# A hybrid encoder layer on one core: the gate table's twelve blocks written out, its stores issued by ScalarE

## The chip, the cores and the metric

The kernel runs on one core of a Trainium2 chip. The metric is the device time of one execution in microseconds (us), lower is better. Before the change it is 3697.43 us, the median of 3 runs (3694.62 to 3698.45).

## The reference

One layer: two token mixers on a shared input projection, a gated merge, and then a retrieval layer of single-neuron experts (PEER) with 128 x 128 experts. The change touches only the last part. For a token with its 8 heads of 16 chosen experts the reference computes

```python
gate = jax.nn.softmax(best_s, axis=-1)
u = expert_u[experts]
v = expert_v[experts]
act = jax.nn.gelu(jnp.einsum('pd,phkd->phk', xb, u), approximate=False)
return jnp.einsum('phk,phkd->pd', (gate * act.astype(f32)).astype(xb.dtype), v)
```

There are 1024 tokens and the width is 1024. An expert's number is i x 128 + j, with i and j from the two halves of the key.

## The kernel before

It runs through phases: front, mixer, merge, route, rows, experts, finish. Of the 1024 tokens, 768 are "dense": for them the kernel computes the activation of every expert (`ahead_dram`, 128 rows of 128 experts) and a table of gates that is nearly all zeros (`gates_dram`, 128 x 128 x 768 floats), and the expert phase later multiplies the two and applies `expert_v`. The other 256 tokens are "sparse": their chosen rows are gathered one by one by indirect DMAs.

The change lies in `rows_phase` (line 1739). All of its stretch runs these streams together:

- **The rows of `expert_u`**, 128 in number. POOL issues the load of a row (512 KB, L1686), ScalarE (ACT) copies the high part (`cut_high`, L1711), VectorE (DVE) subtracts to get the low part (`cut_low`, L1715), TensorE (PE) multiplies in three passes (L460 to L462), 48 matmuls for a row in two halves h = 0 and 1, ACT applies Gelu to each half (`gelu`, L1721), and SP stores that half, 192 KB, into `ahead_dram` (`store`, L1691). The Gelu of a half waits until the store of the same half of the row before has landed (`ge_out[h]`), for there is one buffer `ge` for each half.
- **The sparse tokens**: POOL issues gathers of 128 rows of 4 KB (L1637) into a ring of four buffers, and DVE multiplies each with the tokens (L1654).
- **The gate table**, in twelve blocks of 64 tokens, each of 16 groups of 4 tokens. For a group DVE makes a one-hot of j for four tokens (L2011) and the weighted one-hot of i for three of them (L2015). ACT makes the fourth (`last_row`: L1878, then L1880), one group ahead. PE multiplies the two for each token (L2083, 8 instructions for a group) and then 6 matmuls of a row of `expert_u`. ACT copies the result out of PSUM into `stage` (L1903; the profile calls that memory `arena`). A block takes two rows of `expert_u` with it, numbers 48 to 71 in all. The store of a finished block into `gates_dram` (L1862) is 4096 KB in runs of 64 tokens, 256 bytes.

The rows phase has three parts: eight tiles with the search of the best experts (rows 0 to 47), the twelve blocks, and then the remaining rows 72 to 127 (`rest`), of which the first 23 pairs run with eight gathers each.

The order inside a block on ACT is written by hand: for each group the fourth one-hot of the group after it, then the copy out; the Gelu of the row's first half after the fifth group of its eight (k == 4), the Gelu of its second half after the first group of the next eight (k == 0), and for the last row of the block after the sixteenth group, in the order copy out, Gelu, then the next block's first `last_row`. At the start of a block ACT also waits for the store of the block two before (`st_out`).

On every engine the twelve blocks are a hardware loop of six turns of two blocks each: `blocks` (line 1789) on POOL and PE, `act.Fori` with `link.enter` and `link.leave` on ACT (line 1928) and DVE (line 2041), `sp.Fori` on SP (line 1855). The addresses and the values waited for are computed from the loop's register at every use. SP's list for a block is four `ahead_dram` stores (two rows, two halves), then a wait for the copy out of the block's last group and the block's store:

```python
sp.wait_ge(g_cp.sem, g_cp.done(b * NG + (NG - 1)))
sp.dma_start(gv[:, :, bass.ds(b * BT, BT)],
             stage[:, :, half * BT:(half + 1) * BT]).then_inc(st_out[half].sem, 16)
```

Of the kernel before, what the change touches and what calls it, by code (L numbers as in the profile page):

```python
# [1723 lines left out]
ROWS_BLOCK = 2  # L1724
# [9 lines left out]
def rows_phase(nc, TV, TI, arena, iT, jT, wT, gates, h2hi, h2lo, expert_u, ahead, few, table, keep):  # L1734
# [9 lines left out]
    BT = 64  # L1744
    G = 4
    NG = BT // G
    PER = NG // ROWS_BLOCK
    CH = 2 * KD // PER
    NB = TD // BT
# [4 lines left out]
    with ExitStack() as ctx:  # L1754
# [4 lines left out]
        stage = arena[:, :].rearrange("p (i t) -> p i t", t=2 * BT)  # L1759
# [18 lines left out]
        hot_done, g_mm, g_cp = Steps(sem("hot_done"), 2), Steps(sem("g_mm"), 2), Steps(sem("g_cp"), 2)  # L1778
        st_out = [Steps(sem(f"st_out{i}"), 1, 16) for i in range(2)]
        gv = gates.rearrange("i j t -> j i t")  # L1780

        def tiles(eng, body):

            for t in range(FEW + 1):
                body(t, max(t - FEW, 0) if t >= FEW else DT + t, t < FEW, t == FEW)
            with eng.Fori(FEW + 1, TT) as t:
                body(t, t + (-FEW), False, False)

        def blocks(eng, body):

            with eng.Fori(0, NB // 2) as turn:
                body(turn)

        def rest(eng, body):

            with eng.Fori(0, WITH) as turn:
                body(turn, False, True)
            with eng.Fori(WITH, TURNS - 1) as turn:
                body(turn, False, False)
            body(TURNS - 1, True, False)  # L1800

        with nc.Block() as block:
            @block.gpsimd
            def _(pool):
# [24 lines left out]
                def block_rows(turn):  # L1829
                    for half in range(2):  # L1830
# [3 lines left out]
                        for i in range(RING):  # L1834
                            few.gather(pool, table, batch, half, i)
                            if i % 2 == 0:
                                load(b * 2 + (ROW_GATE + 2 + i // 2), i // 2)

                blocks(pool, block_rows)

                def rest_rows(turn, last, rows):
# [9 lines left out]
            @block.sync  # L1851
            def _(sp):
                with sp.Fori(0, ROW_GATE) as r:
                    A.store(sp, r, r)
                with sp.Fori(0, NB // 2) as turn:
                    for half in range(2):
                        b = turn * 2 + half
                        for j in range(ROWS_BLOCK):
                            A.store(sp, b * 2 + (ROW_GATE + j), b * 2 + (ROW_GATE + j))

                        sp.wait_ge(g_cp.sem, g_cp.done(b * NG + (NG - 1)))
                        sp.dma_start(gv[:, :, bass.ds(b * BT, BT)],  # L1862
                                     stage[:, :, half * BT:(half + 1) * BT]).then_inc(st_out[half].sem, 16)
                with sp.Fori(ROW_REST, NKEYS) as r:
                    A.store(sp, r, r)
                for half in range(2):
                    sp.wait_ge(st_out[half].sem, st_out[half].done(NB // 2 - 1))
                for out in A.ge_out:
                    sp.wait_ge(out.sem, out.done(NKEYS - 1))

            @block.scalar
            def _(act):
                link = Chain(act, sem("act_rows"))

                def last_row(b, gi):
                    at = bass.ds(b * BT + (gi * G + G - 1), 1)
                    w = less[:, bass.ds(b * NG + gi, 1)]
                    link(act.activation(away[:, gi % 2], K.iota[:, :], ACT.Abs, bias=iT[:, at], scale=-1.0))  # L1878
                    act.wait_ge(g_mm.sem, g_mm.free(b * NG + gi))
                    act.activation(row[:, gi % 2 * G + G - 1], away[:, gi % 2], ACT.Relu, bias=wT[:, at], scale=w).then_inc(hot_last.sem, 1)  # L1880

                def tile(t, at, sparse, first):
                    for j in range(R):
                        r = t * R + j
                        A.cut_high(act, r + 1, 1 - j % 2, (t * (R // 2) + (j + 1) // 2) * 16 + 16)
                        for h in range(2):
                            A.gelu(act, r, h)
                        if j == R // 2:
                            act.wait_ge(bm_done, t + 1)
                            act.activation(best[:, :, :], best[:, :, :], ACT.Exp).then_inc(be_done, 1)  # L1890

                def block_rows(turn):
                    for half in range(2):
                        b = turn * 2 + half

                        act.wait_ge(st_out[half].sem, st_out[half].free(turn))
                        last_row(b, 0)
                        for gi in range(NG):
                            if gi + 1 < NG:
                                last_row(b, gi + 1)  # L1900
                            at = half * BT + gi * G
                            act.wait_ge(g_mm.sem, g_mm.done(b * NG + gi))
                            act.activation(stage[:, :, at:at + G], pg[gi % 2][:, :, :].rearrange("p t i -> p i t"), ACT.Copy).then_inc(g_cp.sem, 1)  # L1903
                            j, k = divmod(gi, PER)
                            r = b * 2 + (ROW_GATE + j)
                            if k == 0 and gi:
                                A.gelu(act, r + (-1), 1)
                            if k == 1:
                                A.cut_high(act, r + 1, 1 - j, (b + (ROW_GATE // 2 + j)) * 16 + 16)
                            if k == 4:  # L1910
                                A.gelu(act, r, 0)
                        A.gelu(act, b * 2 + (ROW_GATE + ROWS_BLOCK - 1), 1)

                def rest_rows(turn, last, rows):
                    for p in range(2):
                        r = turn * 2 + (ROW_REST + p)
                        if not (last and p):
                            A.cut_high(act, r + 1, 1 - p, (turn + (ROW_REST // 2 + p)) * 16 + 16)
                        for h in range(2):
                            A.gelu(act, r, h)  # L1920
                    if last:
                        act.wait_ge(few.row_used.sem, few.row_used.done(ITEMS - 1))
                        act.activation(few.dot[:, :, :], few.dot[:, :, :], ACT.Gelu).then_inc(act_done, 1)

                A.cut_high(act, 0, 0, 16)
                tiles(act, tile)
                act.wait_ge(turned_done, DT)
                with act.Fori(0, NB // 2) as turn:
                    link.enter(turn, 2 * NG)
                    block_rows(turn)  # L1930
                link.leave(NB // 2)
                rest(act, rest_rows)

            @block.vector
            def _(dve):
                link = Chain(dve, sem("dve_rows"))
# [66 lines left out]
                def block_rows(turn):  # L2003
                    for half in range(2):
                        b = turn * 2 + half
                        for gi in range(NG):
                            u = gi % 2

                            dve.wait_ge(g_mm.sem, g_mm.free(b * NG + gi))
                            four = jT[:, bass.ds(b * BT + gi * G, G)]  # L2010
                            dve.tensor_tensor(col[:, u * G:(u + 1) * G], K.iota[:, None, :].to_broadcast([P, G, P]),  # L2011
                                              four[:, :, None].to_broadcast([P, G, P]), ALU.is_equal)
                            for q in range(G - 1):
                                at = bass.ds(b * BT + (gi * G + q), 1)
                                step = dve.tensor_scalar(row[:, u * G + q], K.iota[:, :], iT[:, at], wT[:, at], ALU.is_equal, ALU.mult)  # L2015
                            step.then_inc(hot_done.sem, 1)
                            if gi % RING == RING - 1:
                                i = gi // RING
                                few.dot_row(dve, b * RING + (ITEMS_BEST + i), i)
                            j, k = divmod(gi, PER)  # L2020
                            if k == 4:
                                A.cut_low(link, b * 2 + (ROW_GATE + j + 1), 1 - j)
# [15 lines left out]
                    tile(turn + (FEW + 1), turn + 1, False, False)  # L2038
                link.leave(DT - 1)
                turned(TT - 1, DT - 1)  # L2040
                with dve.Fori(0, NB // 2) as turn:
                    link.enter(turn, 2 * ROWS_BLOCK)
                    block_rows(turn)
                link.leave(NB // 2)
                with dve.Fori(0, WITH) as turn:
                    link.enter(turn, 2)
                    rest_rows(turn, False, True)
# [10 lines left out]
            def _(pe):  # L2058
# [35 lines left out]
                tiles(pe, tile)  # L2094
                turn_over(TT - 1)
                blocks(pe, block_rows)
                rest(pe, rest_rows)

# [282 lines left out]
```

## Time and profile before

| | us |
|---|---|
| median of 3 runs | 3697.43 |
| the profiled execution, its own time | 3682.71 |
| its span | 3681.0 |
| PE busy | 3360.2 |
| DVE busy | 2580.8 |
| ACT busy | 1181.7 |
| the twelve blocks, first to last PE instruction of the table | 1627.9 to 2060.5 |

The profiled execution is 14.7 us shorter than the median of the runs. Times in the trace are counted from the start of its span. An engine's idle time is put down to what ended it: another engine's instruction, a DMA, or "issue", which is time in which the profile shows nothing that the engine waited for. An instruction on a queue (SPq, ACTq) is the issue of a DMA, not the transfer.

### The profile page before, as it was taken

To read this page: it belongs to the slowest core of one execution; us is meant where nothing else is said; L and a number is where in the kernel's file an instruction comes from. 1 tells how busy PE (TensorE), PEld (TensorE's weight loads), DVE (VectorE), ACT (ScalarE), POOL (GpSimd) and SP (SyncE) were. 2 spreads that over 40 slices of the span, in tenths; PEclk is the share of its full clock that TensorE was granted. 3 is DMA by queue.
4 is the path that set the end of the run, shared out by engine and by line. 5 is a ranking of instruction groups with operands and counts; after the bars stand their busy time and mean duration, and the time that the engine had idled before them with its cause. 6 is when DMAs were issued, how large, how long until landed. Compare 5 with 4: busy or idle time off the path is not lost. (4 is left out here: it accounts for less than half of the span.)

```text
span 3681.0 us, 58605 instructions
## 1 busy us (share of the span) xinstructions
PE 3360.2 (91%) x18867; PEld 3062.0 (83%) x18867; DVE 2580.8 (70%) x4927; ACT 1181.7 (32%) x2017; POOL 873.6 (24%) x904
## 2 busy tenths in 40 slices
PE   5997999799698899998989799998799999999996
PEld 4997888788587899998888799998688888888885
DVE  6435777455588788988878566661777777777775
ACT  3003555433222222247667322222222222222220
POOL 1000111111000011122212266661333333333331
PEclk8998999899899899999999899999899999999998
DMA  6622222253110344448888899993887787787875
GB/s 251 220 92 97 85 77 87 88 153 120 58 44 28 102 152 144 136 140 226 226 221 222 260 343 346 339 338 112 290 289 291 282 295 286 283 295 282 293 286 192
DMA packets 435649, 742.47 MB, mean 202 GB/s; under 512 B 224368, under 2 KB 275744, under 8 KB 432416
## 3 DMA queue, kind: packets, MB, share of 16 engines
q1 hardware_dynamic: 335200, 369.32, 30.4%
q0 software_dynamic: 98624, 369.14, 29.0%
q10 hardware_dynamic: 1664, 2.13, 0.2%
q8 instruction: 68, 1.11, 0.1%
q14 instruction: 93, 0.76, 0.1%
HBM read 607.30 MB, written 133.19 MB: 201 GB/s over the span
## 5 line engine op out<-in xcount | busy, mean ns | idle before, releaser
L460 PE MATMUL apab<-h2hi,auhib 128*128 128x384 f32 x2048 | 709.7, 347 | 64.2 <-DVEq L60 42.4
L461 PE MATMUL apab<-h2lo,auhib 128*128 128x384 f32 x2048 | 690.1, 337 | 0.0
L462 PE MATMUL apab<-h2hi,aulob 128*128 128x384 f32 x2048 | 689.8, 337 | 0.0
L1637 POOL DMA_INDIRECT vrow<-in_expert_v,fw_now x256 | 318.8, 1245 | 723.5 <-DVE acc L1663 710.4
L460 PEld LDWEIGHTS apab<-h2hi,auhib 128*128 128x128 f32 x2048 | 389.7, 190 | 71.9 <-ACT ageb L1721 31.6
L461 PEld LDWEIGHTS apab<-h2lo,auhib 128*128 128x128 f32 x2048 | 389.6, 190 | 0.0
L462 PEld LDWEIGHTS apab<-h2hi,aulob 128*128 128x128 f32 x2048 | 388.5, 190 | 0.0
L1721 ACT ACTIVATE ageb<-apab 128x384 f32<-128x384 f32 x256 | 125.7, 491 | 683.4 <-PE apab L462 633.9
L2245 PE MATMUL eheld<-vhi,Hhi 128*128 128x512 f32 x768 | 303.3, 395 | 31.8 <-DVE Hlo L2203 31.8
L1663 DVE SCALAR_TENSOR_TENSOR acc<-vrow,fw_share,acc 128x1024 f32<-128x1024 f32 x256 | 327.3, 1279 | 0.0
L1686 POOL DMA_DIRECT2D aurb<-in_expert_u x128 | 71.7, 560 | 1050.2 <-DVEq L60 732.7
L2217 DVE TENSOR_TENSOR acc<-acc,evo 128x512 f32<-128x512 f32 x192 | 132.2, 688 | 257.3 <-PE evo L2247 257.3
L2179 ACT ACTIVATE Hhi<-gr 128x768 fp32r<-128x768 f32 x128 | 108.5, 848 | 606.4 <-DVE gr L2195 606.4
L2246 PE MATMUL eheld<-vlo,Hhi 128*128 128x512 f32 x768 | 300.4, 391 | 0.0
L2247 PE MATMUL eheld<-vhi,Hlo 128*128 128x512 f32 x768 | 299.6, 390 | 0.0
L2245 PE MATMUL evo<-vhi,Hhi 128*128 128x512 f32 x768 | 298.8, 389 | 0.0
L2246 PE MATMUL evo<-vlo,Hhi 128*128 128x512 f32 x768 | 298.8, 389 | 0.0
L2247 PE MATMUL evo<-vhi,Hlo 128*128 128x512 f32 x768 | 298.7, 389 | 0.0
L2083 PE MATMUL gp<-grow,gcol 128*128 128x128 f32 x1536 | 213.6, 284 | 42.9 <-ACT grow L1880 33.3
L2083 PEld LDWEIGHTS gp<-grow,gcol 128*128 128x128 f32 x1536 | 203.1, 197 | 54.2 <-issue 40.3
L1715 DVE TENSOR_TENSOR aulob<-aurb,auhib 128x1024 fp32r<-128x1024 f32 x128 | 156.5, 1223 | 114.4 <-ACT auhib L1711 108.9
L1654 DVE SCALAR_TENSOR_TENSOR urow<-urow,nx 128x1024 f32<-128x1024 f32 x128 | 156.6, 1226 | 68.3 <-DMA urow<-in_expert_u_rows,fw_now 58.8
(309 smaller groups left out, 7376.4 us busy)
## 6 DMA issues: line engine op xcount, KB each, us to landing
aurb<-in_expert_u POOLq DMA_DIRECT2D x128, 512.0 KB
vraw<-in_expert_v SPq DMA_DIRECT2D x128, 512.0 KB, 3.3
ahead_dram<-ageb SPq DMA_DIRECT2D x256, 192.0 KB
gates_dram<-arena SPq DMA_DIRECT2D x12, 4096.0 KB, 24.4
ga<-ahead_dram SPq DMA_DIRECT2D x128, 384.0 KB, 5.4
gr<-gates_dram SPq DMA_DIRECT2D x128, 384.0 KB, 6.0
late<-in_w_ada SPq DMA_DIRECT2D x48, 512.0 KB, 6.4
gw<-in_w_in POOLq DMA_DIRECT2D x8, 1408.0 KB
```

What stands on the lines that cost most here:

```text
L460: pe.matmul(out, lhi, rhi, start=(k == 0), stop=False)
L461: pe.matmul(out, lhi, rlo, start=False, stop=False)
L462: return pe.matmul(out, llo, rhi, start=False, stop=(k == n - 1))
L1637: pool.indirect_dma_start(self.ring[i], None, table, bass.IndirectOffsetOnAxis(ap=self.now[:, h, i:i + 1], axis=0)).then_inc(self.row_in[i ...
L1654: dve.scalar_tensor_tensor(self.ring[i], self.ring[i], 1.0, self.h2[:, i % FEW], ALU.mult, ALU.mult, accum_out=flat[:, bass.ds(n, 1)]).the ...
L1663: dve.scalar_tensor_tensor(at, self.ring[i], flat[:, bass.ds(n - ITEMS, 1)], at, ALU.mult, ALU.add).then_inc(self.row_used.sem, 1)
L1715: link(link.eng.tensor_tensor(self.ulo[:, p], self.ur[:, p], self.uhi[:, p].bitcast(F32), ALU.subtract), self.ulo_done.sem)
L2083: step = pe.matmul(pg[u][:, q], col[:, u * G + q], row[:, u * G + q], start=True, stop=True)
L2217: dve.tensor_tensor(place_of(u), place_of(u), vo[u // 2 % BANKS][:, :], ALU.add).then_inc(vo_add.sem, 1)
L2245: pe.matmul(bank[:, :], hi, vhi[:, m, ds], start=fresh, stop=False)
L2246: pe.matmul(bank[:, :], hi, vlo[:, m, ds], start=False, stop=False)
L2247: step = pe.matmul(bank[:, :], lo, vhi[:, m, ds], start=False, stop=(q == Q - 1 and (dh == 1 or final)))
```

## The change

Three edits. `blocks`, used by POOL and PE, becomes a Python loop, so the six turns are written out as straight code and `turn` is a number: addresses and values waited for are constants. ACT, DVE and SP get the same, and the chain of ACT and DVE drops its `enter` and `leave`. The store of a finished block moves from SP's list to ACT's, between the copy out of the block's last group and the Gelu of its last half row.

```diff
         def blocks(eng, body):
 
-            with eng.Fori(0, NB // 2) as turn:
+            for turn in range(NB // 2):
                 body(turn)
...
                     A.store(sp, r, r)
-                with sp.Fori(0, NB // 2) as turn:
+                for turn in range(NB // 2):
                     for half in range(2):
                         b = turn * 2 + half
                         for j in range(ROWS_BLOCK):
                             A.store(sp, b * 2 + (ROW_GATE + j), b * 2 + (ROW_GATE + j))
 
-                        sp.wait_ge(g_cp.sem, g_cp.done(b * NG + (NG - 1)))
-                        sp.dma_start(gv[:, :, bass.ds(b * BT, BT)],
-                                     stage[:, :, half * BT:(half + 1) * BT]).then_inc(st_out[half].sem, 16)
...
                             if k == 4:
                                 A.gelu(act, r, 0)
+                        act.wait_ge(g_cp.sem, g_cp.done(b * NG + (NG - 1)))
+                        act.dma_start(gv[:, :, bass.ds(b * BT, BT)],
+                                      stage[:, :, half * BT:(half + 1) * BT]).then_inc(st_out[half].sem, 16)
                         A.gelu(act, b * 2 + (ROW_GATE + ROWS_BLOCK - 1), 1)
...
-                with act.Fori(0, NB // 2) as turn:
-                    link.enter(turn, 2 * NG)
-                    block_rows(turn)
-                link.leave(NB // 2)
+                blocks(act, block_rows)
...
-                with dve.Fori(0, NB // 2) as turn:
-                    link.enter(turn, 2 * ROWS_BLOCK)
-                    block_rows(turn)
-                link.leave(NB // 2)
+                blocks(dve, block_rows)
```

## Rows read from the trace of the kernel before

**Rows 1.** The page's first line.

```profile
span 3681.0 us, 58605 instructions
```

**Rows 2.** Busy time in stretches of 73 us, one turn: engines, granted clock, DMA share, GB/s.

```profile
1700.00:1773.00 73.00, 65.49 (x450) 63.59 (x451) 59.15 (x148) 51.61 (x111) 16.07 (x14) 0.97 0.84 225
1992.00:2065.00 73.00, 68.11 (x468) 66.53 (x469) 58.02 (x145) 51.66 (x109) 15.55 (x15) 0.98 0.85 228
```

**Rows 3.** Waits, 1627 to 2065 us: total us, times, longest.

```profile
PEld gp L2083 <- issue: 40.3, 12, 5.5
PE gp L2083 <- ACT grow L1880: 33.3, 11, 5.2
DVE gcol L2011 <- issue: 14.1, 5, 3.0
ACT gaway L1878 <- issue: 13.2, 5, 3.3
```

**Rows 4.** Timeline of PE: start, length in us, and in brackets the idle time before.

```profile
1700.48 2.07 PE L2083 MATMUL gp<-grow,gcol 128*128 128x128 f32 x8 [4.56 <-ACT grow L1880]
1736.00 1.15 PE L2083 MATMUL gp<-grow,gcol 128*128 128x128 f32 x8 [1.77 <-ACT grow L1880]
1772.48 2.07 PE L2083 MATMUL gp<-grow,gcol 128*128 128x128 f32 x8 [4.16 <-ACT grow L1880]
1809.16 1.94 PE L2083 MATMUL gp<-grow,gcol 128*128 128x128 f32 x8 [1.77 <-ACT grow L1880]
```

**Rows 5.** Timeline of ACT around the ends of blocks and at a ninth group.

```profile
1660.82 0.60 ACT L1903 ACTIVATE arena<-gp 128x512 f32<-128x512 f32 x1 [1.33 <-PE gp L2083]
1661.87 0.49 ACT L1721 ACTIVATE ageb<-apab 128x384 f32<-128x384 f32 x1 [0.45 <-PE apab L462]
...
1681.32 0.49 ACT L1721 ACTIVATE ageb<-apab 128x384 f32<-128x384 f32 x1
...
1699.11 0.40 ACT L1878 ACTIVATE gaway<-iota,iT 128x128 f32<-128x128 f32 x1 [2.66 <-issue]
1699.75 0.49 ACT L1880 ACTIVATE grow<-gaway,wT,gless 128x128 f32<-128x128 f32 x1 [0.23 <-ACT gaway L1878]
```

**Rows 6.** Granted clock and busy time after a turn's end.

```profile
1698.00:1710.00 12.00, 9.52 (x59) 9.53 (x60) 7.92 (x20) 7.61 (x17) 0.00 (x0) 0.86 0.98 216
```

**Rows 7.** Register instructions of DVE's sequencer for the weighted one-hots: ns min/median/max.

```profile
L2015 DVEq FUSED_REGOPS  x576: 46/69/81, 1626.4 to 2057.4; - x192
```

**Rows 8.** Instruction fetch, 1627 to 2065 us: packets, MB, share of the DMA engines.

```profile
q14 instruction: 56, 0.46, 0.3%
```

**Rows 9.** DMAs that ACT issues in the merge phase: ns min/median/max.

```profile
L1255 ACTq DMA_DIRECT2D mwr<-in_w_branch x4: 424/492/565, 719.5 to 721.0; - x4
```

**Rows 10.** Timeline of SP, DMA issues: start and how long SP was in it.

```profile
1663.13 0.39 SPq L1862 DMA_DIRECT2D gates_dram<-arena  x1
1673.70 12.10 SPq L1691 DMA_DIRECT2D ahead_dram<-ageb  x1
...
1697.22 0.38 SPq L1862 DMA_DIRECT2D gates_dram<-arena  x1
1711.97 4.42 SPq L1691 DMA_DIRECT2D ahead_dram<-ageb  x1
...
2064.06 0.38 SPq L1862 DMA_DIRECT2D gates_dram<-arena  x1
2066.70 28.14 SPq L1691 DMA_DIRECT2D ahead_dram<-ageb  x1
```

**Rows 11.** The gate table's stores, L1862.

```profile
DMA to landing us min/median/max: 23.4/24.4/24.9
```

**Rows 12.** Timelines of ACT and PE after the last block.

```profile
2097.35 0.98 ACT L1721 ACTIVATE ageb<-apab 128x384 f32<-128x384 f32 x2 [25.70 <-DMA ahead_dram<-ageb]
2097.89 0.69 PE L460 MATMUL apab<-h2hi,auhib 128*128 128x384 f32 x1 [19.40 <-ACT ageb L1721]
```

**Rows 13.** Busy time, clock, DMA share and GB/s after the last block.

```profile
2065.00:2095.00 30.00, 13.50 (x78) 13.18 (x77) 11.32 (x18) 1.93 (x3) 11.00 (x12) 0.79 1.08 321
2095.00:2120.00 25.00, 22.11 (x114) 22.11 (x115) 13.02 (x19) 5.92 (x9) 11.77 (x12) 0.84 0.69 214
2120.00:2484.00 364.00, 355.04 (x2013) 349.45 (x2012) 250.80 (x372) 82.39 (x126) 241.30 (x248) 1.00 0.96 343
```

## The prediction

> **What bounds the kernel now.** I read first the page, whose span is 3681.0 us [rows 1], then the busy times of the stretch of the twelve blocks, turn by turn. There PE is busy 65.5 of 73 us, DVE 59.2 and ACT 51.6; the last turn, with no jump back behind it, has 68.1 [rows 2]. So PE is the bound of this stretch, and what can be won is its idle time and the time it runs at the lower clock. Then I read the waits of the stretch. PE was held 11 times by ACT's one-hot, 33.3 us in all, and ACT and DVE each stood five times for "issue", 13.2 and 14.1 us [rows 3]: five is the number of jumps back in six turns. The timeline puts them in place: PE's gap at the start of a turn is 4.56 and 4.16 us, and between the two blocks of a turn 1.77 us [rows 4]. Six gaps of 1.77 are 10.6 us, which leaves 22.7 us for five jumps, 4.54 each, in line with the two shown. ACT's own line shows why a jump costs more: after the last Gelu it has 2.66 us of "issue" ahead of the next one-hot, and PE starts when that and the weighted one-hot are done [rows 5].
>
> Last I read SP's line and what follows the last block. The store of a block takes SP only 0.38 us, but the next store of SP stands in its issue until 1685.80, which is 22.7 us after the block's store was issued, in the other block 19.2 us (1716.39 less 1697.22), and after the last one 30.8 us (2094.84 less 2064.06) [rows 10]; the block's store lands after 24.4 us [rows 11]. So the issue of SP's next DMA ends shortly before the long store does. Within the blocks nobody waits for SP. After the last block somebody does: ACT's Gelu waits 25.70 us for the landing of that delayed store and PE 19.40 us for the Gelu [rows 12].
>
> **The change, part by part.**
>
> *Jumps back.* Five gaps of 4.54 us become gaps like those between blocks, 1.77 us, since the same instructions stand there: 5 x 2.77 = 13.9 us. The same gap is the price if nothing but the jump goes, and I see no way for it to be longer than now for that reason.
>
> *The clock after the gap.* The first eight table instructions after a jump take 2.07 us instead of 1.15 [rows 4], and the granted clock of the 12 us around a turn's start is 0.86 [rows 6]: PE, having stood 4.56 us, ran a while at the lower of its two levels, 1.2 instead of 2.4 GHz. What it costs: the block from 1736.00 to the gap before 1772.48 (at 1768.32) takes 32.32 us; the one from 1700.48 to 1734.23 takes 33.75, the one from 1772.48 to 1807.39 takes 34.91. That is 1.4 and 2.6 us, say 1.94 for each of five, 9.7 us. But at 1809.16 the clock fell behind a gap of only 1.77 us (1.94 us for eight), in one of six such places, so I count five sixths: 8.1 us. Bounds 0 and 9.7.
>
> *Constants.* The register instructions go (69 ns each on DVE's sequencer [rows 7]). DVE shows its idle time as waits for others or for the jumps, and PE is the bound: 0 us, covered by DVE's own work. If the cover were gone DVE would still be issued ahead of its need. POOL and SP have long waits in this stretch and get nothing from it.
>
> *ACT's new work.* Twelve times ACT waits for its own copy and issues a DMA before the Gelu. The copy ends at 1661.42 and the Gelu starts at 1661.87 [rows 5], so 0.45 us are free. A DMA issued by ACT took 0.49 us [rows 9], and a wait for ACT's own instruction before cost 0.23 us [rows 5]: 0.72 less 0.45 is 0.27 us, which delays the Gelu, behind it the first one-hot of the next block, and PE. Twelve times: 3.2 us lost. Bounds: 0, and 0.565 + 0.23 = 0.8 us with nothing free, 9.5 us. SP loses the same wait and issue, at no gain.
>
> *After the last block.* If SP's short stores no longer stand behind the long one, the wait of 19.40 us goes, with about 2 us of low clock. What is late next is DMA: between 2065 and 2095 its engines are full (share 1.08 by this view), and from 2120 to 2484, where the gathers end, the share is 0.96 with PE losing 9 us [rows 13]. The bytes to be moved are the same. The stall wasted only what the engines left idle behind it, 25 us at 0.69 instead of 0.96 or so, 25 x 0.27 = 6.8 us. I take 7 us; the bounds are 0 (SP stands all the same) and 21 us (DMA is no limit). Near the DMA bound, because 0.96 is nearly full. The Trainium skill (DMA: Bandwidth & Descriptors, Issuing engines are not separate DMA queues) says that DMAs from several engines run on the same 16 DMA engines and that issuing from several saves only the initiating sequencer's time, which is usually small. By that rule this part is worth 0 and the time would be 7 us above mine. Here that time is no small one: SP was 28.14 us in one issue [rows 10].
>
> Sum: 13.9 + 8.1 - 3.2 + 7 = 25.8 us. Against the profiled execution of 3682.7 that is 3656.9; the median of the runs stands 14.7 us above that execution, and I give the forecast against it: 3697.4 - 25.8 = 3671.6, so **3672 us**. Its own range: the least is 13.9 + 0 - 9.5 + 0 = 4.4 us won, the most 13.9 + 9.7 - 0 + 21 = 44.6, which is 3653 to 3693.
>
> **The rivals.**
>
> *A, ends slower: the long store holds SP's short ones from ACT's list too.* What stands in the issue for 12 and 28 us may be the list of SP alone or something that SP and ACT share. The trace has no long store issued by one engine and a short one by the other, so it can't say. If shared, the order has become worse: now SP issues the last half row before the block's store, afterwards ACT issues the block's store first. The store of that half row then stands until 19.2 to 22.7 us after ACT's issue at about 1661.65, so until 1680.9 or 1684.3, and lands 2.5 us later (2097.35 less 2094.84 [rows 10, 12]): 1683.4 or 1686.8. The Gelu that needs its buffer starts now at 1681.32 [rows 5]. ACT would stand 2.1 or 5.5 us in every block; PE feels it less what ACT is ahead (about 1 us) but falls to the lower clock behind the longer ones (1.9 us). I take 3 us for each of 11 blocks, 33 us, bounds 0 and 5.5 + 1.9 = 7.4, 81 us; and the 7 us of the tail don't come. 3672 + 7 + 33 = 3712 us. It decides from the point where PE loses more than 18.8 / 11 = 1.7 us in a block. For it speaks that SP's wait follows the long store's progress and not SP's own work. Against it that the known wait is of one list behind itself. The Trainium skill (DMA: Bandwidth & Descriptors, Queues, rings and completion order) says that SP and ACT each own a ring on every DMA engine, but no descriptor generator of their own; by the first half A falls, by the second it can stand, and no row here shows it.
>
> *B: straight code has to be fetched too.* In the loop 56 packets of instructions came, 0.46 MB [rows 8], about 9 in a turn, and only at the jump was anybody seen standing for "issue". Straight code needs about as many bytes on ACT and DVE and more on PE, whose code now stays. If the fetch is merely late at other places, the first two terms are lost and the time is 3697.4 + 3.2 - 7 = 3694 us. Against it: inside a turn, whose code is fetched in order, these rows show no such wait.
>
> *C: the moved store does nothing and the rest holds.* 3679 us; it lies inside the range of the forecast.
>
> **How the numbers follow.** The forecast (C inside it) 0.56, A 0.34, B 0.10. A measurement of this kernel can tell about 0.2%, 7.4 us, from no change. The forecast is nearly always beyond that on the fast side. A, between 3679 and 3760, gives faster in one of six, the same in one of five, and slower else. B is mostly the same. Faster: 0.54 + 0.05 + 0.02 = 0.61; slower 0.22 + 0.02 = 0.24; the same 0.15. The range has to hold most of both signs: from 3654, where nearly all of the forecast's range starts, to 3724, which takes in the greater part of A.
>
> **What would show it.** Right: ACT and DVE have no "issue" waits in the twelve blocks; PE's gaps at the eleven block ends are about 2.0 us; the granted clock of the stretch is above 0.97; a block takes some 34.4 us; SP's issues stay below 1 us while ACT's long store is under way; PE's wait of 19.4 us is gone and the DMA share stays near 0.96 through 2120. A is shown by SP issues of 10 to 20 us, by ACT's Gelu of the ninth group waiting for a landing of `ahead_dram`, and by PE gaps in the tenth or eleventh group. B is shown by "issue" waits within blocks. The forecast is wrong if ACT itself stands in the issue of its DMA for more than 1 us, or if the tail stays.

## The result and the profile after

The changed kernel takes 3642.91 us, the median of 4 runs (3638.2 to 3650.44), before 3697.78 us (4 runs). The ratio is 0.9866, 95% interval 0.9841 to 0.9891: 54.9 us faster by the medians. The forecast was 3672 us, within 3654 to 3724. The side was right, the size was a little under half of what came, and the time lies below the range.

The profiled execution of after takes 3640.8 us, 41.9 us less than the one of before (3682.7). Where that lies is read from two groups, the table's matmuls and the first matmuls of the expert phase; the last pair of each row is its first and last start. Before, first:

```profile
L2245 PE MATMUL eheld<-vhi,Hhi x768: 389/389/767, 2597.0 to 3645.1; 128*128 128x512 f32 x192
```

and after (line numbers are lower by 6 below the edits):

```profile
L2077 PE MATMUL gp<-grow,gcol x1536: 272/275/422, 1633.7 to 2031.4; 128*128 128x128 f32 x192
L2239 PE MATMUL eheld<-vhi,Hhi x768: 387/389/764, 2555.6 to 3603.3; 128*128 128x512 f32 x192
```

The table's matmuls ran from 1627.9 to 2060.5 before. So there are three stretches. Up to the first block after is 5.8 us later, in code that the change doesn't touch (over all runs here this start lies anywhere between 1628 and 1656 us). The **twelve blocks** went from 432.6 to 397.7 us, 34.9 less. **From the last block to the expert phase** it went from 536.5 to 524.2 us, 12.3 less. The rest is equal within 0.5 us. The two stretches of the forecast, 18.8 and 7 us there, gave 47.2 us together.

The waits within the blocks, 1634 to 2032 us (total us, times, longest), answer to [rows 3]:

```profile
ACT arena L1900 <- PE gp L2077: 82.1, 156, 2.0
DVE gcol L2008 <- PE gp L2077: 41.7, 47, 2.2
PE gp L2077 <- DVE grow L2012: 18.3, 12, 2.9
PE gp L2077 <- issue: 1.5, 1, 1.5
DVE gcol L2008 <- DVE aulob L1715: 0.5, 1, 0.5
```

Every "issue" wait of ACT and DVE is gone. PE is held for 2.9 us before the first block, once for 0.3 us inside it, and for 1.5 us at each of the eleven block ends (one of them stands in the row with "issue"). The same view of before has two rows more that matter, which I hadn't used:

```profile
PE gp L2083 <- DVE grow L2015: 9.5, 24, 3.2
DVE gcol L2011 <- DVE aulob L1715: 8.0, 24, 0.3
```

These are short waits inside the blocks. Without the one of 3.2 us ahead of the first block PE lost 6.3 us in 23 of them, and DVE stood 0.33 us behind each of its 24 subtractions (L1715), where it waits for its own completion. After, one of each is left, in the first block.

PE's busy time in all of the stretch, before and after, with the granted clock and the DMA share:

```profile
1628.00:2061.00 433.00, 393.39 (x2685) 382.28 (x2685) 353.16 (x884) 302.65 (x643) 95.73 (x85) 0.96 0.80 214
```

```profile
1634.00:2032.00 398.00, 381.07 (x2686) 370.87 (x2685) 350.79 (x884) 302.38 (x643) 67.02 (x84) 1.00 0.86 233
```

The same 2685 matmuls were busy for 12.3 us less, mostly since PE never fell to 1.2 GHz here (clock 0.96, now 1.00). Not all of it is clock: a kernel below (ACT's straight code alone) keeps the short waits at a clock of 0.99, and PE is busy 382.9 us there, so some 2 us of the 12.3 can come without the lower clock. The 34.9 us are these 12.3 us of busy time and 22.6 us of gaps: 5 x (4.54 - 1.51) = 15.2 at the jumps, 6 x 0.26 = 1.6 at the other block ends, and some 6 us of short waits.

A block's end on ACT, and PE's next gap, answering to [rows 4, 5], with DVE's last one-hots for the next block:

```profile
1666.35 0.60 ACT L1900 ACTIVATE arena<-gp 128x512 f32<-128x512 f32 x1 [1.34 <-PE gp L2077]
1666.98 0.40 ACTq L1910 DMA_DIRECT2D gates_dram<-arena  x1
1667.05 0.85 DVE L2012 TENSOR_SCALAR grow<-iota,iT,wT 128x128 f32<-128x128 f32 x3
1667.48 0.49 ACT L1721 ACTIVATE ageb<-apab 128x384 f32<-128x384 f32 x1 [0.53 <-PE apab L462]
1667.87 0.39 ACT L1875 ACTIVATE gaway<-iota,iT 128x128 f32<-128x128 f32 x1
1668.30 0.49 ACT L1877 ACTIVATE grow<-gaway,wT,gless 128x128 f32<-128x128 f32 x1
```

```profile
1668.89 1.13 PE L2077 MATMUL gp<-grow,gcol 128*128 128x128 f32 x8 [1.52 <-DVE grow L2012]
```

The copy ends at 1666.95, the issue starts 0.03 us later and is over at 1667.38, ahead of the Gelu: it fits into the time that was free. Between the two one-hot steps no wait is left; before there were 0.23 us [rows 5]. The profile names DVE's one-hot as what released PE, but by the same rows DVE's was over at 1667.90 and ACT's at 1668.79, 0.1 us before PE starts. An experiment below shows that it was ACT.

SP's short stores over the whole kernel, min/median/max in ns, and the long store's time to landing, answering to [rows 10, 11]:

```profile
L1691 SPq DMA_DIRECT2D ahead_dram<-ageb x256: 332/332/369, 1228.1 to 2524.0; - x128
```

```profile
DMA to landing us min/median/max: 23.7/26.5/76.4
```

No short store stood in its issue for more than 0.369 us. The last long store took 76.4 us to land. And behind the last block, to be read beside [rows 13]:

```profile
2035.00:2060.00 25.00, 25.00 (x146) 25.00 (x145) 16.33 (x24) 5.87 (x9) 14.77 (x16) 1.00 1.10 377
2060.00:2120.00 60.00, 58.40 (x334) 57.46 (x333) 40.47 (x62) 13.75 (x21) 40.87 (x41) 1.00 1.05 380
```

PE is busy for all of the first 25 us while the DMA engines move 377 GB/s, where before, with PE standing, they moved 321.

### The profile page after: what moved, and what is told of

Its sections match the earlier page's. It is cut to its first block and busy times, and to the rows that moved or that the text cites. A ratio compares the mean times of both kernels' runs of the same rounds, so it can differ in the third digit from the quotient of the medians.

```text
span 3639.1 us, 56033 instructions
## 1 busy us (share of the span) xinstructions
PE 3352.0 (92%) x18867; PEld 3052.5 (84%) x18867; DVE 2578.6 (71%) x4927; ACT 1181.3 (32%) x2017; POOL 865.3 (24%) x904
## 5 line engine op out<-in xcount | busy, mean ns | idle before, releaser
L2077 PE MATMUL gp<-grow,gcol 128*128 128x128 f32 x1536 | 206.5, 278 | 19.8 <-DVE grow L2012 18.3
L1715 DVE TENSOR_TENSOR aulob<-aurb,auhib 128x1024 fp32r<-128x1024 f32 x128 | 156.4, 1222 | 89.2 <-ACT auhib L1711 85.8
```

The source lines that it names most:

```text
L1715: link(link.eng.tensor_tensor(self.ulo[:, p], self.ur[:, p], self.uhi[:, p].bitcast(F32), ALU.subtract), self.ulo_done.sem)
L2077: step = pe.matmul(pg[u][:, q], col[:, u * G + q], row[:, u * G + q], start=True, stop=True)
```

## The experiments

All kernels keep what is computed. "Blocks" is from the first to the last start of a table matmul, "to experts" from there to the first start of the expert phase's matmul; both are read from the two groups as above. The kernels came in three lots, each on one chip; before was timed beside them at 3696.1 us (13 runs), 3690.3 (1) and 3701.4 (6). Where a kernel ran once, its total also holds the start of the blocks, which lies between 1629.5 and 1654.2 us in those traces; its stretches say more than its total.

**Before again.** No edit.

> The kernel before once more, to have its trace from the chip of the three other runs. The profiled execution of before was 14.7 us shorter than the median of its runs, the one of after was not. If the stretches of the trace are stable, the twelve blocks take 432 to 434 us again and the stretch from the last table instruction to the first matmul of the expert phase 535 to 540 us. If the missing 13 us (54.9 measured against 41.9 between the two traces) lie in these stretches, one of them comes out 10 us longer.

```profile
L2083 PE MATMUL gp<-grow,gcol x1536: 271/275/574, 1629.5 to 2058.7; 128*128 128x128 f32 x192
L2245 PE MATMUL eheld<-vhi,Hhi x768: 389/389/763, 2592.9 to 3640.0; 128*128 128x512 f32 x192
```

Blocks 429.2 us, to experts 534.2 us, and 3677.58 us in all, while 13 other executions of the same kernel on this chip took 3689.89 to 3702.68. So the traces of before are stable within 3 us in each stretch, and the profiled execution is again the shortest, by 12 to 25 us. The missing 13 us are in neither trace. They stay open. Against this trace of before, the blocks of after are 31.5 us shorter instead of 34.9.

**Straight code alone.** SP keeps the long stores.

```diff
                             A.store(sp, b * 2 + (ROW_GATE + j), b * 2 + (ROW_GATE + j))
 
+                        sp.wait_ge(g_cp.sem, g_cp.done(b * NG + (NG - 1)))
+                        sp.dma_start(gv[:, :, bass.ds(b * BT, BT)], ...)
...
-                        act.wait_ge(g_cp.sem, g_cp.done(b * NG + (NG - 1)))
-                        act.dma_start(gv[:, :, bass.ds(b * BT, BT)], ...)
```

> The straight code alone: SP keeps the stores of the table. Theory 1 (the two parts of the change act apart, jumps and constants within the blocks, the moved store behind them): the twelve blocks take about 397 us as in after, SP's short stores stand 10 to 23 us in their issue, PE has the stall of about 19 us after the last block, and the stretch from there to the expert phase is back at 536 us; about 12 us slower than after, 3655 us. Theory 2 (a part of what was won within the blocks comes from SP's short stores being free): the twelve blocks take 403 us or more.

Measured: 3663.12 us (4 runs), ratio to before 0.9904 (0.9886 to 0.9922). Blocks 397.6 us, to experts 541.2. SP's line and PE's and ACT's after the last block:

```profile
2038.82 0.43 SPq L1862 DMA_DIRECT2D gates_dram<-arena  x1
2042.68 28.22 SPq L1691 DMA_DIRECT2D ahead_dram<-ageb  x1
```

```profile
2073.65 0.69 PE L460 MATMUL apab<-h2hi,auhib 128*128 128x384 f32 x1 [19.18 <-ACT ageb L1721]
```

All of the gain in the blocks comes from the straight code, and the stall behind them stays as it was. Theory 1 holds. SP's short store is free at 2070.90, 32.1 us after the long store's issue, which lands after 33.7 us. By the medians the straight code alone is worth 33.0 us of the 3696.1.

Here the stretch to the experts is 4.7 us longer than in the first trace of before. What differs behind the stall is PE's wait for the signal of DVE's subtraction (L60 is the helper that gives it). It is 6.6 us in before (2098 to 2560 us), 12.8 in this kernel (2074 to 2540) and 13.6 in after (2031 to 2520), in the same order:

```profile
PE apab L460 <- DVEq L60: 6.6, 10, 2.0
PE apab L460 <- DVEq L60: 12.8, 14, 2.4
PE apab L460 <- DVEq L60: 13.6, 16, 2.2
```

So against this kernel the moved store brings 541.2 less 524.2, 17.0 us of the stretch, and 20.2 us by the medians: about the whole stall.

**The moved store alone.** The loops stay.

```diff
-                        sp.wait_ge(g_cp.sem, g_cp.done(b * NG + (NG - 1)))
-                        sp.dma_start(gv[:, :, bass.ds(b * BT, BT)], ...)
...
+                        act.wait_ge(g_cp.sem, g_cp.done(b * NG + (NG - 1)))
+                        act.dma_start(gv[:, :, bass.ds(b * BT, BT)], ...)
                         A.gelu(act, b * 2 + (ROW_GATE + ROWS_BLOCK - 1), 1)
```

> The moved store alone, in the loops as before. Theory 1: the twelve blocks take 433 to 436 us (ACT's issue adds 0 to 0.3 us a block), the stall of 19 us after them is gone and the stretch to the expert phase takes 524 us; 3683 to 3688 us. Theory 2: the blocks are shorter than 430 us. Rival A of the prediction would show SP issues of 10 to 20 us here as well; the trace of after has none above 1.2 us, so I expect none.

Measured: 3688.07 us (10 runs), ratio 0.9983 (0.9963 to 1.0002). To experts 524.4 us as expected, but blocks 438.6 us, 2.6 above the expectation and 6 to 9 more than in the two traces of before. ACT at a block's end:

```profile
1661.69 0.60 ACT L1900 ACTIVATE arena<-gp 128x512 f32<-128x512 f32 x1 [1.33 <-PE gp L2083]
1662.45 0.41 ACTq L1910 DMA_DIRECT2D gates_dram<-arena  x1
1662.99 0.49 ACT L1721 ACTIVATE ageb<-apab 128x384 f32<-128x384 f32 x1 [0.70 <-PE apab L462]
1663.38 0.39 ACT L1875 ACTIVATE gaway<-iota,iT 128x128 f32<-128x128 f32 x1
1664.00 0.49 ACT L1877 ACTIVATE grow<-gaway,wT,gless 128x128 f32<-128x128 f32 x1 [0.23 <-ACT gaway L1875]
```

```profile
1664.72 1.15 PE L2083 MATMUL gp<-grow,gcol 128*128 128x128 f32 x8 [2.02 <-ACT grow L1877]
```

In the loop the issue begins 0.16 us after the copy instead of 0.03, the Gelu comes 0.25 us later than before, and PE's gap is 2.02 instead of 1.77 us. This is the cost that the prediction had for the whole change (0.27 us a block). At the five jumps it is more: gaps of 5.29 to 5.46 us, 5.35 in the mean instead of 4.54, for ACT's "issue" there is 3.1 to 3.3 us instead of 2.3 to 3.3. That makes 5 x 0.81 + 6 x 0.23 = 5.4 us in all. The cost is real in a loop and absent in straight code. So the two parts are not independent: alone, the move isn't clear of no change.

**Eleven stores by SP, the last by ACT.**

```diff
+                        if b < NB - 1:
+                            sp.wait_ge(...); sp.dma_start(...)
...
+                        if b == NB - 1:
+                            act.wait_ge(...); act.dma_start(...)
```

> Straight code, SP issues eleven of the stores and ACT only the last. Theory 1: SP's short stores stand 10 to 23 us in the blocks and nobody waits for them, the blocks take 397 us, and since the last store is ACT's the stall after the blocks is gone, 524 us to the expert phase: the same as after, 3643 us. If stores standing in the blocks cost something, it is between after and the straight code alone.

Measured: 3643.96 us (4 runs), ratio 0.9858 (0.9841 to 0.9875), the same as after. Blocks 397.7 us, to experts 521.4. SP stood 10.8 to 13.0 us in the issue of a short store behind each of its long ones and nobody waited for it. The whole worth of the move, 19.2 us against the straight code alone (3663.12), lies in the last store.

**Which engine's straight code?** Three kernels, all with the moved store, to be compared with its 438.6 us. PE, POOL and SP keep their loops.

```diff
-                with act.Fori(0, NB // 2) as turn:
-                    link.enter(turn, 2 * NG)
-                    block_rows(turn)
-                link.leave(NB // 2)
+                for turn in range(NB // 2):
+                    block_rows(turn)
```

> The moved store, and only ACT's twelve blocks as straight code; PE, DVE, POOL and SP keep their loops. Theory 1a (PE's gap at a jump is ACT's chain: its jump, then its one-hot): the gaps at the jumps shrink from 4.5 us to at most what DVE and PE need for their own jumps, about 2.5 to 3.5 us, since DVE's 3.0 us of issue lie ahead of its one-hots; gaps between the blocks of a turn 1.5 us. The blocks take 422 to 428 us. Theory 1b (all engines' jumps end together): they stay above 4 us.

> The moved store, and only DVE's twelve blocks as straight code. Theory 1a: the gaps at the jumps stay at 4.2 to 5.2 us and those between blocks at 1.8, for ACT is last there, but PE's short waits of 0.27 us for DVE's one-hots inside the blocks vanish, and so do DVE's own waits of 0.33 us behind cut_low, worth 0.5 us a block: 427 to 430 us. If the constants of DVE are worth nothing, 433 us or more.

> The moved store, ACT and DVE as straight code; PE, POOL and SP keep their loops. If PE's own jump is hidden in the 1.5 us gap and its register instructions cost nothing, the blocks take 397 to 400 us as in after. If PE's jump shows, gaps of 1.5 us become 2.5 to 3.5 us at five places: 402 to 408 us.

One run each. ACT alone: 3645.32 us, blocks 408.6 us, better than expected (422 to 428). DVE alone: 3684.34 us, blocks 432.0 us, a little above the expectation. Both: 3633.95 us, blocks 399.6 us, as in after within 2 us. The waits of the first two:

```profile
PE gp L2081 <- DVE grow L2013: 17.6, 29, 3.2
PE gp L2081 <- ACT grow L1877: 11.6, 7, 1.7
DVE gcol L2009 <- issue: 10.0, 4, 3.0
DVE gcol L2009 <- DVE aulob L1715: 8.0, 24, 0.3
```

```profile
PE gp L2081 <- ACT grow L1877: 38.0, 11, 5.3
PE gp L2081 <- DVE grow L2015: 3.3, 2, 3.0
DVE gcol L2011 <- DVE aulob L1715: 0.5, 1, 0.5
```

With ACT straight no gap at a block's end is above 2.44 us, although DVE still jumps and stands 3 us for "issue" there. DVE runs ahead of PE, so most of its jump is covered. With DVE straight the gaps at the jumps stay at 4.9 to 5.3 us, but PE's short waits within the blocks vanish with DVE's own. PE's jump, POOL's and SP's cost next to nothing together. Of the 40.9 us between the blocks of the loops with the moved store and those of after, ACT's straight code brings 30.0, about three quarters, and DVE's on top of it 9.0.

**Four blocks a turn.** Three turns, two jumps back instead of five, all registers as before.

```diff
-            with eng.Fori(0, NB // 2) as turn:
-                body(turn)
+            with eng.Fori(0, NB // 4) as turn:
+                for part in range(2):
+                    body(turn * 2 + part)
```

> The moved store, all engines in loops of three turns of four blocks: two jumps back instead of five, all register addresses as before. If a jump costs 2.8 us of gap and 1.9 us of low clock, three fewer make the blocks 14 us shorter than with two blocks a turn, about 419 us; gaps of 1.77 us stay between blocks and so do the waits of 0.27 us. If the price lies in the fetch of the loop's code, it grows with the body and the two jumps left cost more than 4.5 us each.

Measured, one run: 3683.12 us, blocks 421.5 us. Three jumps fewer make the blocks 17.1 us shorter, 5.7 us for a jump, where the prediction had 2.77 + 1.94 = 4.7; with the moved store in the loop a jump's gap is 3.35 us longer than another block's end (5.35 and 2.00). The two that are left cost gaps of 4.9 and 5.3 us, no more than the 5.3 to 5.5 with the shorter body, so no growth of the price with the body's length shows, from two to four blocks. What a jump waits for the runs don't say. The rows of the waits:

```profile
PE gp L2086 <- ACT grow L1878: 28.2, 11, 5.3
ACT gaway L1876 <- issue: 5.9, 2, 3.2
```

**After again.** No edit, as the neighbour of the last three.

> The changed kernel once more, beside the two that follow on the same chip: 3640 to 3650 us, the twelve blocks 397.7 us, 524 us from them to the expert phase.

3644.67 us (4 runs, 3637.24 to 3667.72), blocks 397.7, to experts 521.9.

**The next block's one-hot ahead.** ACT makes it before the last copy, the store and the last Gelu of a block.

```diff
-                        last_row(b, 0)
+                        if b == 0:
+                            last_row(b, 0)
                         for gi in range(NG):
                             if gi + 1 < NG:
                                 last_row(b, gi + 1)
+                            elif b + 1 < NB:
+                                last_row(b + 1, 0)
```

> The changed kernel, and ACT makes the first weighted one-hot of the next block ahead of the last copy of the block, the store and the last Gelu. If the gap of 1.5 us at each block end is ACT's chain (Gelu, then two one-hot steps), it goes to 0 to 0.3 us: 11 x 1.3 = 14 us off the twelve blocks, 383 to 385 us. If the trace is right that DVE's one-hot releases PE there, the gaps and the 397.7 us stay.

Measured: 3630.02 us (4 runs, 3620.05 to 3639.03), ratio to before 0.9792 (0.9739 to 0.9844); after is 3644.67 beside it. Blocks 378.2 us:

```profile
L2080 PE MATMUL gp<-grow,gcol x1536: 272/275/426, 1655.7 to 2033.9; 128*128 128x128 f32 x192
```

```profile
1656.00:2034.00 378.00, 377.65 (x2683) 370.45 (x2681) 350.81 (x884) 300.62 (x642) 66.53 (x83) 1.00 0.90 244
```

PE is busy 377.65 of 378 us, and all gaps at block ends are gone, 19.5 us in the blocks where 14 were expected: 16 us of gaps, and PE is busy 3.4 us less than in after for the same work. DVE's order wasn't touched. So the gap was ACT's chain, and the row that names DVE's one-hot was wrong about the releaser: DVE's part had been done 1.0 us before PE started. The blocks are clearly shorter; by the medians of the whole kernel this one is 14.7 us faster than after, but its runs spread over 19 us and overlap those of after.

**The last store late.** ACT issues it behind the rows that run with gathers.

```diff
+                        if b < NB - 1:
+                            act.wait_ge(...); act.dma_start(...)
...
+                with act.Fori(0, WITH) as turn:
+                    rest_rows(turn, False, True)
+                act.dma_start(gv[:, :, bass.ds((NB - 1) * BT, BT)], stage[:, :, BT:2 * BT]).then_inc(st_out[1].sem, 16)
+                with act.Fori(WITH, TURNS - 1) as turn:
+                    rest_rows(turn, False, False)
```

> The changed kernel, with the last block's store issued only after the 46 rows that run with gathers, where the DMA engines are mostly idle. Theory D (the stretch with gathers is bound by DMA, as I had said of it): the store's share of about 20 us of DMA work leaves it, and the stretch from the blocks to the expert phase goes from 524 to 504 to 510 us. Theory E (PE bounds that stretch, the long store is served in between): 520 to 524 us, the same as after within 0.2%.

Measured: 3644.97 us (4 runs), the same as after; to experts 523.6 us. The 88 us behind the last block, here and in the run of after beside it:

```profile
2032.00:2120.00 88.00, 87.38 (x507) 87.07 (x507) 57.08 (x85) 22.32 (x34) 57.26 (x59) 1.00 0.95 331
```

```profile
2030.00:2118.00 88.00, 86.65 (x497) 85.70 (x496) 57.21 (x85) 21.78 (x33) 56.46 (x58) 1.00 1.05 371
```

Without the long store the engines move 331 GB/s and PE is 0.7 us busier; with it they move 371. The store is carried nearly free. Theory E holds: PE is busy 87.38 of 88 us, and a DMA share of 0.95 didn't limit it. Over the whole stretch to the experts PE still waits 13.3 us for DVE's signal, about as in after.

**DVE's wait for itself.** The moved store in the loops; in the blocks DVE's subtraction signals directly and nothing waits for DVE's own completion, and with it `link.enter` and `link.leave` of DVE's loop go too.

```diff
-                                A.cut_low(link, b * 2 + (ROW_GATE + j + 1), 1 - j)
+                                r, p = b * 2 + (ROW_GATE + j + 1), 1 - j
+                                dve.wait_ge(A.uhi_done.sem, A.uhi_done.done(r))
+                                dve.tensor_tensor(A.ulo[:, p], ...).then_inc(A.ulo_done.sem, 1)
```

> The moved store in the loops as before (438.6 us for the blocks), and DVE's subtraction in the blocks signals by its own semaphore, without DVE's wait for its own completion against a register's value. If PE's waits of 0.27 us, twice in a block, come from that wait (DVE idle 0.33 us behind it), they vanish as with DVE's straight code: 432 us. If they come from the register addresses of the one-hots, they stay.

Measured, one run: 3667.81 us, blocks 424.2 us, where 432 were expected. The short waits vanish, only one of DVE's one-hots still holds PE:

```profile
PE gp L2083 <- ACT grow L1877: 38.0, 11, 5.3
PE gp L2083 <- DVE grow L2015: 3.2, 1, 3.2
```

The one-hots still take their addresses from registers here, and DVE's other waits are still against a register's value. So it was DVE's wait for itself, and not the addresses; with straight code the same wait stands against a constant and costs nothing. The blocks became 14.4 us shorter, more than the 6.4 us of waits; PE's busy time also fell, from 394.2 to 386.8 us, at a clock of 0.97 instead of 0.96. Why the clock held better here than with DVE's straight code (394.6 us) the runs don't say.

## Why the forecast had the side and not the size

The first pair of traces gives 47.2 us for the two stretches, where the sum had 25.8. The 21.4 us between them are four terms: some 9 us for the constants, which were put at 0, 5.3 us after the last block, 4.2 us of PE's busy time, and the 3.2 us of ACT's new work that didn't come.

**Jumps back, 13.9 us.** Right in place and mechanism: ACT's jump sets PE's gap, and the issue waits are gone. Measured at the jumps 5 x 3.03 = 15.2 us, of which 13.9 are the jump and 1.3 the shorter block end.

**The clock, 8.1 us.** Too small: PE's busy time fell by 12.3 us, of which at least 10 are the clock. I had taken one sixth off for gaps of 1.77 us that let the clock fall. With gaps of 1.5 us none did, neither here nor in the other straight kernels with those gaps (clock 1.00 in each), so the five jumps gave their full 9.7 us or so, and the slow stretch at 1809.16 [rows 4], which I hadn't counted as a gain, went too.

**"Constants: 0 us, covered by DVE's own work."** This step failed. I read the register instructions as the price of a register and found them covered. The price was in an engine's waits for its own completion, where their value came from a register: 0.33 us behind each of DVE's 24 subtractions, which PE felt as 0.27 us about twice a block, 6 us in all, and 0.23 us between ACT's two one-hot steps, which no engine covers at a block's end; the block ends became 0.26 us shorter, 2.9 us over eleven. For DVE an experiment shows it; for ACT it is read from the traces alone. Both stood in the view that I had open, the first as a row of 8.0 us put down to DVE itself, the second in [rows 5]. That DVE stands for itself isn't cover; the sum needed the question of who waits behind it.

**ACT's new work, -3.2 us.** The price was right for a block's end inside a turn of the loop (2.02 for 1.77 us), too small at its jumps (5.35 for 4.54), and wrong for what was built: in straight code it is 0, and the gap is 1.50 us without it and 1.51 with it. I had priced the wait with the 0.23 us of a register's wait and then put it into code without registers.

**After the last block, 7 us.** "What is late next is DMA" failed. The stretch gave 12.3 us, and moving the long store out of it altogether gave nothing more. I took a share of 0.96 for full, and 321 GB/s at a share of 1.08 [rows 13] for what the engines can do. They did 377 to 380 GB/s. The last store gave way instead and landed after 76.4 us, which nobody waits for. Of the stall's 19.4 us 12.3 came off the stretch in this pair of traces. The other 7 stand in the rows above: PE's waits for DVE's signal are 13.6 us in after and 6.6 in the first trace of before. They are no price of the move, for the straight code with SP's stores has 12.8 us of them; against that kernel the move gave 17.0 to 19.8 us. Why before has fewer is open. My reading that SP's next issue ends shortly before the long store lands did hold for the last store too, though [rows 11] couldn't show it: 32.1 and 33.7 us with the straight code alone.

**The rivals.** A fell: ACT's long store didn't hold a single short store of SP. With the first half of the rule of the Trainium skill (DMA: Bandwidth & Descriptors, Queues, rings and completion order), that each has its own rings, the trace agrees: no issue of SP above 0.369 us. The rule of the Trainium skill (DMA: Bandwidth & Descriptors, Issuing engines are not separate DMA queues), by which issuing from several engines saves only the sequencer's time, usually a small one, agrees where nobody waits (eleven of the stores) and not for the last: 3663.12 against 3643.96 us with only that one issued by ACT. B fell: no issue wait of ACT or DVE within the blocks, and 397.6 or 397.7 us for them in each of the five straight kernels with ACT's old order. C, that the move does nothing, fell as well: straight code alone came to 3663.12 us, and the move took it to 3642.91.

In sum, the two traces and the runs account for 47.2 us of the two stretches against 25.8. The medians differ by 54.9, since the profiled execution of before is shorter than its other runs, twice; the prediction noted the 14.7 us and carried them over to the changed kernel, whose profiled execution is 2 us below its median. The two kernels in loops with several runs have profiled executions 11 to 18 us below their medians, the straight ones from 12 below to 8 above. Whether it is the loop that costs more in the other executions no trace here shows.

## What to carry to other kernels

Where a jump back costs PE more than its own time, look for the engine with no lead over the bound, and write out that engine's loop first: here ACT's alone brought 30 of the 41 us between the loop and the straight code. Price an added instruction in the form of code that it will stand in; behind a wait on the engine's own completion 0.2 to 0.3 us stood idle in the loops and next to nothing in straight code. And a DMA share near 1 is no proof of a DMA bound: ask whether some transfer in it can be late.

## What the runs showed of the hardware that I had not expected

A store in 256-byte runs (4096 KB), issued by SP, held SP's next DMA for 3 to 28 us, in the issue instruction itself; issued by ACT, it held none of SP's (at most 0.369 us). Whether its size or its short runs do it was not varied. Within the blocks the store took 23 to 27 us to land; beside loads and gathers the last one took 33.7 us where PE stood for 19 of them and 76.4 us with PE busy, and there it raised the total from 331 to 371 GB/s. And in the trace a gap of 1.5 us was put down to DVE, whose work had been done for 1.0 us; moving ACT's one-hot showed whose it was.
